# Decode attention kernel: the latent cache is loaded with four tokens to a partition, 3 KB a piece on 32 partitions, instead of one token to a partition

## The chip, the cores and the metric

The kernel runs on one core of one Trainium2 chip. The metric is the device time of one execution in microseconds (us). Engine names are those of the profile: PE is the matrix engine, PEld its weight loads, DVE, ACT and POOL are the vector, scalar and general engines, and SP is the engine that does nothing here but issue transfers (SPq in the rows).

## What is computed

One layer of a hybrid decoder, for a prompt of 1,024 tokens and for eight decode sequences ("rows" of a batch; here called sequences) of four new tokens each, over a past of 2,048 tokens that lies in a paged cache. Of this only the second attention of the decode matters for the change. Its cache holds 192 numbers for a token, 128 of a latent vector and 64 of a rotated key, and page_table says which 16 pages of 128 tokens a sequence owns:

```
past_mla = cache_mla_l[page_table].reshape(Bd, PAST_LEN, KV_LORA + ROPE_DIM)
full_mla = jnp.concatenate([past_mla, mla_row], axis=1)
o_lat = mla_attend(q_lat, q_rope, full_mla[..., :KV_LORA], full_mla[..., KV_LORA:], pos, ...)

def mla_attend(q_lat, q_rope, ckv, k_rope, q_pos, k_pos):
    s = (jnp.einsum('bthr,blr->bhtl', q_lat, ckv)
         + jnp.einsum('bthe,ble->bhtl', q_rope, k_rope)).astype(jnp.float32) * scale
    p = masked_softmax(s, (k_pos[None, :] <= q_pos[:, None])[None, None])
    return jnp.einsum('bhtl,blr->bthr', p.astype(ckv.dtype), ckv)
```

All 2,048 past tokens are visible to every new token, and no term of the score depends on where a past token stands. So the sum over past tokens may be taken in any order, if scores and values use the same one.

## The kernel before

The program is written engine by engine, with semaphores between them. It runs the prompt first (projection, attention, output projection, to about 880 us of the span), then the eight decode sequences one after the other, in a loop over `b` on each engine, and a short output projection for the decode at the end. There is no scheduler: each engine runs its instructions in the order in which the code lists them.

All loads of the decode are issued by SP. For a sequence `b` SP waits until sequence `b - 2` has been finished on PE (semaphore `s_avd`), since the two buffers of each kind alternate (`b % 2`). Then it issues in this order: 16 pages of the other cache (`load_pages`, 256 KB each, into `NSA`), the state of the window (`load_window`, 512 KB, into `WND`), 256 KB of prepared queries (`load_keyed`), 16 pages of the latent cache (`load_latent`, 96 KB each, into `MLD`), and two stores of the window (`store_window`). The page's number is read from a register, so each page has a transfer and some register work of its own. For sequence 0 the same functions are called from the output projection of the prompt (`sp_out`), `load_latent` in its tile 5.

`MLD[b % 2]` has for each of 128 partitions 16 slots of 192 numbers. Two places read it. On DVE, `latent_turns(b)` (L2796) waits for all 16 transfers (`s_ml`) and then turns blocks of 32x32 of it into `MLT` for the scores, by three instructions; it stands in DVE's order behind the last copy of compressor chunks of sequence `b` (L2725, chunk V3), and the whole softmax work of sequence `b` is queued behind it. PE needs its result in `latent_scores` (L2592). On PE, `latent_values` (L2631) multiplies slot `n` of `MLD` by column block `n` of the probabilities, on all 128 partitions. Both take slot and partition as they come: the score of the token in slot n of partition p ends in place (n, p) of the probabilities, and meets the same slot and partition in `latent_values`.

The other cache is needed at its first chunk: PE's `chunk(b, "K0")` (L2339) waits for the 16 transfers of `load_pages`, and stands in PE's order behind the selected scores (L2605) of the sequence before.

Of the kernel before, what the change touches and what calls it, by code (L numbers as in the profile page):

```python
# [20 lines left out]
P = 128  # L21
# [93 lines left out]
def build(nc, x_prompt, x_sample, cache_nsa, cache_mla, state_win, page_table, c_prompt, c_sample,  # L115
# [3 lines left out]
    with ExitStack() as ctx:  # L119
# [34 lines left out]
        def view(off, n):  # L154
            return AR[:, off:off + n]
# [1415 lines left out]
        for u, (kind, i, half, heads, k0, nb, og) in enumerate(UNITS):  # L1571
# [5 lines left out]
            n = len(CH_OF[u])  # L1577
# [454 lines left out]
        def sp_out(sp, tiles, at):  # L2032
            for m, j in enumerate(tiles, at):
                if m >= 2:
                    sp.wait_ge(s_g2, 2 * (m - 1))
                if m >= 1:
                    sp.dma_start(XO[m % 2][0:rows(j), :], x_t[j]).then_inc(s_xo[m % 2], 16)
                if m == 1:
                    load_bias(sp)
                if m == 2:  # L2040
                    load_queries(sp)
                    load_compressors(sp)
                    load_gates(sp)
                if m == 3:
                    pages = page_numbers(sp, 0)
                    load_pages(sp, 0, pages, 0, 8)
                if m == 4:
                    load_pages(sp, 0, pages, 8, NPG)
                if m == 5:
                    load_latent(sp, 0, pages)  # L2050
                if 3 <= m <= 6:
                    keyed_store(sp, m - 3)
                if m == 6:
                    load_keyed(sp, 0)
                    load_window(sp, 0)
                    store_window(sp, 0)
                if m > at:
                    sp.wait_ge(s_yo, m)
                    sp.dma_start(y_t[tiles[m - 1 - at]], YO[(m - 1) % 2][0:rows(tiles[m - 1 - at]), :])\
                        .then_inc(s_out[(m - 1) % 2], 16)  # L2060
# [152 lines left out]
        MLD = [view(o, 3072).rearrange("p (n c) -> p n c", n=NPG) for o in (16384, 38304)]  # L2213
# [266 lines left out]

        def load_latent(sp, b, pages):
            for n in range(NPG):
                sp.dma_start(MLD[b % 2][:, n, :], cache_mla[0, bass.ds(pages[n], 1)].rearrange("o t c -> (o t) c"))\
                    .then_inc(s_ml[b % 2], 16)

        def load_window(sp, b):
# [11 lines left out]
        def sp_decode(sp):  # L2498
            load_mask(sp)
            for b in range(1, NB):  # L2500
                pages = page_numbers(sp, b)
                if b == 1:
                    sp.wait_ge(s_yT, NT)
                load_pages(sp, b, pages, 0, NPG)
                if b == 1:
                    load_late(sp)
                    sp.wait_ge(s_yo, NT)
                    sp.dma_start(y_t[NT], YO[1]).then_inc(s_out[1], 16)
                load_window(sp, b)
                load_keyed(sp, b)  # L2510
                load_latent(sp, b, pages)
                store_window(sp, b)
            sp.wait_ge(s_avd, 8 * (NB - 2) + 8)
            load_weights(sp, WOUT2)
            sp.wait_ge(s_r, 2 * NB)
            for c in range(4):
                at, cs = RS * c, slice(256 * c, 256 * c + 256)
                for b in range(NB):
                    sp.dma_start(GPS[at + TS * b:at + TS * b + TS, :], gate_dram[b:b + 1, cs].to_broadcast([TS, 256]))\
                        .then_inc(s_gps, 16)  # L2520
                sp.dma_start(XOS[at:at + RS, :], x_t[0][:, cs]).then_inc(s_gps, 16)
                sp.dma_start(GFS[at:at + RS, :], g_final[256 * c:256 * c + 256].rearrange("(o n) -> o n", o=1)
                             .to_broadcast([RS, 256])).then_inc(s_gps, 16)
# [540 lines left out]
```

## Time and profile before

| | |
|---|---|
| median of 3 runs | 1114.52 us (1111.03 to 1114.62) |
| profiled execution, its own time | 1115.21 us |
| its span in the trace | 1113.2 us |
| mean granted clock of PE | 0.991 of full speed |
| busy: PE, DVE, ACT, POOL | 97%, 56%, 33%, 8% of the span |
| moved by DMA | 120.25 MB, 108 GB/s over the span |

The profile is of one execution. The span is the time from its first to its last instruction; the execution's own time is 2.0 us longer. Start times in rows count from the start of the span. "Landing" of a transfer counts from its issue to its last byte. A DMA share is the mean busy share of the core's 16 DMA engines; in a short window it can read slightly over 1.

### The profile page before, as it was taken

To read this page: it belongs to the slowest core of one execution; us is meant where nothing else is said; L and a number is where in the kernel's file an instruction comes from. 1 tells how busy PE (TensorE), PEld (TensorE's weight loads), DVE (VectorE), ACT (ScalarE), POOL (GpSimd) and SP (SyncE) were. 2 spreads that over 40 slices of the span, in tenths; PEclk is the share of its full clock that TensorE was granted. 3 is DMA by queue.
4 is the path that set the end of the run, shared out by engine and by line. 5 is a ranking of instruction groups with operands and counts; after the bars stand their busy time and mean duration, and the time that the engine had idled before them with its cause. 6 is when DMAs were issued, how large, how long until landed. Compare 5 with 4: busy or idle time off the path is not lost. (4 is left out here: it accounts for less than half of the span.)

```text
span 1113.2 us, 22587 instructions
## 1 busy us (share of the span) xinstructions
PE 1075.2 (97%) x8368; PEld 763.3 (69%) x8368; DVE 624.6 (56%) x1627; ACT 362.5 (33%) x893; POOL 86.5 (8%) x184
## 2 busy tenths in 40 slices
PE   6899999999999999998999999999999999999997
PEld 3455599998886677776776657664544576777775
DVE  0645323463423477769677766742323588888883
ACT  0322001121112475546555555631112133333330
POOL 0210100110000011101101010011000200000000
PEclk9899999999999999999999999999999999999998
DMA  9933270001006240000000000005794467878781
GB/s 355 310 115 94 72 211 2 16 19 72 1 1 122 44 116 2 1 1 2 1 2 1 2 1 2 1 1 119 169 307 152 142 217 262 271 274 275 261 251 51
DMA packets 96612, 120.25 MB, mean 108 GB/s; under 512 B 31569, under 2 KB 65380, under 8 KB 95480
## 3 DMA queue, kind: packets, MB, share of 16 engines
q1 hardware_dynamic: 96504, 118.81, 34.4%
q8 instruction: 68, 1.11, 0.4%
q14 instruction: 40, 0.33, 0.1%
HBM read 104.41 MB, written 14.36 MB: 107 GB/s over the span
## 5 line engine op out<-in xcount | busy, mean ns | idle before, releaser
L549 PE MATMUL PS<-AR 128*128 128x256 f32 (+2 forms) x896 | 219.7, 403 | 0.0
L549 PEld LDWEIGHTS PS<-AR 128*128 128x128 f32 x896 | 167.8, 190 | 45.2 <-issue 6.2
L2090 PE MATMUL PS<-AR 128*128 128x512 f32 x256 | 112.3, 592 | 0.0
L1747 PE MATMUL PS<-CA,AR 128*128 128x128 f32 x704 | 111.4, 282 | 0.8 <-ACT AR L1821 0.8
L963 DVE TENSOR_TENSOR AR<-PS,AR 128x256 f32<-128x256 f32 (+2 forms) x80 | 36.2, 452 | 134.4 <-PE PS L549 134.3
L1747 PEld LDWEIGHTS PS<-CA,AR 128*128 128x128 f32 x704 | 77.0, 143 | 44.6 <-issue 31.7
L1821 ACT ACTIVATE AR<-PS 128x512 f32<-128x512 f32 (+1 forms) x108 | 58.2, 546 | 125.1 <-PE PS L1747 124.5
L1725 PE MATMUL PS<-AR 128*128 128x65 f32 (+1 forms) x688 | 89.3, 271 | 0.0
L2090 PEld LDWEIGHTS PS<-AR 128*128 128x128 f32 x256 | 47.5, 190 | 54.0 <-issue 54.0
L1725 PEld LDWEIGHTS PS<-AR 128*128 128x128 f32 x688 | 84.3, 192 | 0.0
L1806 ACT ACTIVATE AR<-PS,SM_ 128x512 f32<-128x512 f32 (+4 forms) x192 | 76.6, 471 | 15.9 <-DVE SM_ L1914 8.8
L1700 PE MATMUL PS<-AR 64*128 64x512 f32 (+3 forms) x384 | 74.1, 491 | 6.6 <-ACT AR L1803 3.9
L1835 DVE COPY AR<-PS 128x512 f32<-128x512 f32 (+1 forms) x100 | 57.3, 586 | 15.5 <-PE PS L1747 15.1
L1803 ACT ACTIVATE AR<-PS,SM_ 128x512 f32<-128x512 f32 (+2 forms) x80 | 51.5, 655 | 15.4 <-DVE SM_ L1914 15.3
L760 ACT ACTIVATE AR<-PS 128x256 f32<-128x256 f32 (+2 forms) x20 | 8.0, 402 | 139.7 <-PE PS L549 98.6
L1876 DVE TENSOR_REDUCE SM_<-PS 128x1 f32<-128x512 f32 (+1 forms) x48 | 29.9, 664 | 41.8 <-PE PS L1696 30.2
L1722 PE MATMUL PS<-AR 128*64 128x128 f32 x656 | 50.0, 282 | 1.2 <-DVE AR L1980 1.2
L2183 DVE TENSOR_TENSOR AR<-PS,AR 128x512 f32<-128x512 f32 x16 | 11.1, 692 | 71.0 <-PE PS L2090 71.0
L541 PE MATMUL PS<-AR 128*64 128x128 f32 x896 | 49.8, 273 | 0.0
L541 PEld LDWEIGHTS PS<-AR 128*64 128x64 f32 x896 | 48.8, 137 | 1.3 <-issue 1.2
L1992 POOL TENSOR_TENSOR AR<-AR 128x256 f32<-128x256 f32 x32 | 23.3, 727 | 326.3 <-DVE AR L1980 325.7
L1700 PEld LDWEIGHTS PS<-AR 64*128 64x128 f32 x384 | 28.9, 185 | 26.3 <-ACT AR L1803 11.9
(364 smaller groups left out, 1622.9 us busy)
## 6 DMA issues: line engine op xcount, KB each, us to landing
AR<-in_cache_nsa SPq DMA_DIRECT2D x128, 256.0 KB, 5.0
AR<-in_cache_mla SPq DMA_DIRECT2D x128, 96.0 KB, 3.7
AR<-in_x_prompt SPq DMA_DIRECT2D x16, 512.0 KB, 4.6
AR<-in_w_ada SPq DMA_DIRECT2D x3, 2048.0 KB, 11.4
AR<-in_w_in SPq DMA_DIRECT2D x6, 1024.0 KB, 8.4
AR<-in_w_ada SPq DMA_DIRECT2D x8, 512.0 KB, 4.3
AR<-in_w_out SPq DMA_DIRECT2D x4, 1024.0 KB, 10.0
AR<-in_w_out SPq DMA_DIRECT2D x2, 2048.0 KB, 17.5
```

The costliest lines, as they stand in the source:

```text
L541: mm = pe.matmul(bank[64 * h:64 * h + 64, P * r:P * r + P], weights[:, k, h, 64 * r:64 * r + 64], tokens[:, k, :], start=(fresh and r == 0 ...
L549: mm = pe.matmul(bank[:, 0:WIDE[g]], tokens[:, k, :], w, start=(fresh and k == 0), stop=(last and k == 3), skip_group_check=True)
L963: return dve.tensor_tensor(out, src, other, ALU.add)
L1700: mm = pe.matmul(scores(u, gi, o, o + P * n), QT[64 * g:64 * g + 64, r, q], keys[64 * g:64 * g + 64, ks], start=True, stop=True)
L1722: mm = pe.matmul(ob[64 * g:64 * g + 64, P * (r % 2):P * (r % 2) + P], (VS1 if kind == "sel" else VW1)[:, kb, g, 0:64], tile, start=(n == 0 ...
L1725: mm = pe.matmul(out, tile, v, start=(n == 0), stop=(n == nb - 1))
L1747: mm = pe.transpose(PS[:, 4 + c % 2, P * (t - t0):P * (t - t0) + P], tile(u, t), ident)
L1803: act.activation(probs(u, gi, lo, hi), sc, ACT.Exp, bias=NM[:, at, gi:gi + 1], scale=-1.0, accum_out=TOT[og % 4][:, slot:slot + 1]).then_i ...
L1806: act.activation(probs(u, gi, lo, hi), sc, ACT.Exp, bias=NM[:, at, gi:gi + 1], scale=-1.0).then_inc(s_exp, 1)
L1821: evac(act, c, lambda o, i: act.activation(o, i, ACT.Copy), s_evA)
L1835: copy(PTB[:, c % 4, 0:nt, :], PS[:, 4 + c % 2, 0:P * nt].rearrange("p (t q) -> p t q", t=nt)).then_inc(done, 1)
L2090: mm = pe.matmul(PS[0:n, 2 + 2 * (m % 2) + c, :], YTO[m % 2][:, f, 0:n], weights[:, f, 512 * c:512 * c + 512], start=(f == 0), stop=(f == 7))
```

## The change

Each page of the latent cache, 128 tokens of 768 bytes that lie one behind the other, was written one token to a partition, into slot n. Now tokens 4h to 4h+3 of page n go to one partition, 4h + n % 4, into the four slots from 4 (n // 4) on. These slots are neighbours, so that the four tokens are one piece of 3,072 bytes on both sides. A transfer has 32 such pieces in place of 128 of 768 bytes, and writes every fourth partition; four pages (n, n+1, n+2, n+3 of one group) together fill the same four slots of all 128 partitions. Nothing else is changed: the same 128 transfers of 96 KB, the same buffer, the same semaphore and count.

```
         def load_latent(sp, b, pages):
             for n in range(NPG):
-                sp.dma_start(MLD[b % 2][:, n, :], cache_mla[0, bass.ds(pages[n], 1)].rearrange("o t c -> (o t) c"))\
+                sp.dma_start(MLD[b % 2][n % 4:P:4, 4 * (n // 4):4 * (n // 4) + 4, :],
+                             cache_mla[0, bass.ds(pages[n], 1)].rearrange("o (h l) c -> (o h) l c", l=4))\
                     .then_inc(s_ml[b % 2], 16)
```

In SP's order, at the loads for sequence 1, the program before reads as follows (AR is the one large on-chip array of which MLD, WND and NSA are views, in_cache_mla is the latent cache; an ISA row is the register work for a page's address, and 128x192 are partitions and numbers of a partition):

```order
L2489 DMA AR<-in_state_win 128x1024
L2387 DMA AR<-sample_q_by_key_weights 128x512
L2483 ISA
L2483 DMA AR<-in_cache_mla 128x192
L2483 ISA
L2483 DMA AR<-in_cache_mla 128x192
```

and the changed program, at the same place:

```order
L2490 DMA AR<-in_state_win 128x1024
L2387 DMA AR<-sample_q_by_key_weights 128x512
L2483 ISA
L2483 DMA AR<-in_cache_mla 32x768
L2483 ISA
L2483 DMA AR<-in_cache_mla 32x768
```

No instruction moved; SP has 712 such rows in both, with the shape of the latent transfers as their only difference. Lines behind L2483 are one higher in the changed program.

In DVE's order, at the turns of sequence 0's latents, the changed program has the rows of the program before (there they are L2725, L2812, L2796, L2833 and L2834), with the same shapes:

```order
L2726 COPY AR<-PS 128x32x16
L2813 STREAM_TRANSPOSE AR<-AR 128x4x4x32
L2797 STREAM_TRANSPOSE AR<-AR 128x16x2x32 x3
L2834 TENSOR_SCALAR AR<-AR 32x127
L2835 TENSOR_TENSOR AR<-PS,CE 128x128
```

Nothing moved here either; the three instructions that wait for the latent transfers read the same 128 partitions and 16 slots.

## Rows read from the trace of the kernel before

**Rows 1.** The page: engines, and the span in 40 slices.

```profile
PE 1075.2 (97%) x8368; PEld 763.3 (69%) x8368; DVE 624.6 (56%) x1627; ACT 362.5 (33%) x893; POOL 86.5 (8%) x184
...
DMA  9933270001006240000000000005794467878781
```

**Rows 2.** Waits, whole span: of seven that name a DMA, largest and smallest.

```profile
engine line waited for: us in total, times, longest us
...
ACT AR L880 <- DMA AR<-in_x_prompt: 23.0, 3, 16.2
...
PE PS L648 <- DMA AR<-in_w_in: 1.7, 1, 1.7
```

**Rows 3.** Waits of DVE alone, 740 to 1113 us, some of twenty.

```profile
DVE AR L2864 <- PE PS L2598: 6.4, 7, 0.9
...
DVE AR L2725 <- PE PS L2339: 5.5, 14, 0.5
```

**Rows 4.** Chain that ended last, one sequence: start, us, engine and line.

```profile
938.54 1.09 PE PS L2543 x64
...
942.33 3.63 PE PS L2592 x8
...
965.01 1.09 PE PS L2543 x64
```

**Rows 5.** SP's timeline, loads for sequences 3 and 4: start, us, line, count.

```profile
938.66 8.66 SPq L2478 DMA_DIRECT2D AR<-in_cache_nsa  x16
947.38 0.43 SPq L2489 DMA_DIRECT2D AR<-in_state_win  x1
947.86 0.43 SPq L2387 DMA_DIRECT2D AR<-sample_q_by_key_weights  x1
948.48 9.14 SPq L2483 DMA_DIRECT2D AR<-in_cache_mla  x16
957.68 0.94 SPq L2495 DMA_DIRECT2D out<-AR  x2
964.68 9.70 SPq L2478 DMA_DIRECT2D AR<-in_cache_nsa  x16
```

**Rows 6.** The readers of these loads, timeline: PE's K0 chunk, DVE's turns.

```profile
957.25 0.60 PE L2339 MATMUL PS<-CA,AR 128*128 128x128 f32 x4
...
965.05 1.08 DVE L2725 COPY AR<-PS 128x512 f32<-128x512 f32 x1 [0.45 <-PE PS L2339]
...
965.98 1.22 DVE L2796 STREAM_TRANSPOSE AR<-AR 128x1024 f32<-128x1024 f32 x1
```

**Rows 7.** Issues and landings of the latent and of the other cache.

```profile
L2483 SPq DMA_DIRECT2D AR<-in_cache_mla x128: 332/333/1355, 823.3 to 1064.6; - x128
...
DMA to landing us min/median/max: 1.9/3.7/6.5
...
L2478 SPq DMA_DIRECT2D AR<-in_cache_nsa x128: 332/333/1692, 802.9 to 1054.6; - x128
...
DMA to landing us min/median/max: 2.6/5.0/7.4
```

**Rows 8.** Windows: us, engines busy, and last granted clock, DMA share, GB/s.

```profile
938.66:960.60 21.94, 21.94 (x245) 15.39 (x230) 17.94 (x42) 4.52 (x10) 1.54 (x3) 1.00 0.95 323
960.60:964.60 4.00, 3.54 (x56) 3.10 (x55) 3.89 (x8) 3.98 (x6) 0.00 (x0) 1.00 0.03 8
...
1045.14:1067.90 22.76, 22.76 (x221) 16.20 (x208) 18.70 (x46) 5.94 (x13) 0.00 (x0) 1.00 0.91 311
```

**Rows 9.** Windows in which one kind of load leads, same columns.

```profile
824.00:832.00 8.00, 8.00 (x23) 3.80 (x22) 1.38 (x2) 0.60 (x1) 0.00 (x0) 1.00 0.82 242
...
784.00:786.00 2.00, 2.00 (x36) 1.07 (x35) 1.03 (x2) 0.00 (x0) 0.00 (x0) 1.00 1.06 182
...
845.90:848.50 2.60, 2.60 (x8) 1.17 (x7) 0.00 (x0) 0.00 (x0) 0.00 (x0) 1.00 0.86 301
911.67:920.80 9.13, 9.13 (x100) 5.73 (x99) 7.98 (x16) 0.88 (x3) 0.00 (x0) 1.00 0.88 291
```

**Rows 10.** DVE's copy of a chunk with no load in flight, timeline.

```profile
963.02 1.06 DVE L2725 COPY AR<-PS 128x512 f32<-128x512 f32 x1
```

## The prediction

> **What bounds the kernel now.** I first read the page. PE is busy for 97% of the span, and the DMA engines are loaded only in parts, with shares of 0.7 to 0.8 in the decode [rows 1]. A load that is shared out so can still be a bound at one place, so the next view is the list of waits: what ended the idle time of an engine. Seven entries name a DMA, and all seven are of the projection in the first part of the span, on x, w_ada, w_in and a constant; the largest is 23.0 us and the smallest 1.7 us [rows 2]. None names the latent cache, and none is of the decode. DVE, which alone waits for the latent transfers directly, waited in the loop over sequences for PE and ACT: at L2864 seven times, 0.9 us at most, and at L2725 0.5 us at most [rows 3]; L2796, where the latents are waited for, is not in the list.
>
> The third view is the chain that ended last. Through a sequence of the decode it goes from PE instruction to PE instruction with a few on DVE, and it repeats: PE's key products start at 938.54 and again at 965.01, so a sequence takes 26.47 us [rows 4]. No transfer stands in it.
>
> The fourth view is SP and the queue, since a hidden load is hidden by a margin, and the change acts on the margin. For one sequence SP issues from 938.66 to 958.62, and the loads of the next sequence start at 964.68 [rows 5]. SP idles some 6 us, waiting for PE to free a buffer. The DMA engines work at a share of 0.95 until 960.60, and then at 0.03 for 4.00 us [rows 8]. So of 26.0 us between the starts of two bursts the queue is full for 21.94, and has 4.1 us to spare; in the last burst it is full for 22.76.
>
> **What the change does, part by part.**
>
> *Issue on SP.* There are as many transfers and register instructions as before. An issue is 332 to 333 ns in the median [rows 7], the same for 128x192 and for 128x512 numbers, so it doesn't follow the size. The 16 take 9.14 us [rows 5], or 0.57 us each with the register work. I take no change. If a transfer of fewer pieces were cheaper to issue, SP would idle longer before its next wait; if each cost 0.3 us more, the 16 would cost 4.8 us, which the 6 us still hold. Both give 0 us on the path. SP's queue behind the latents holds only the two window stores, and then the wait for PE.
>
> *The transfers.* The latents are 16 x 98,304 bytes = 1.57 MB for a sequence. What they cost the queue now is best seen at sequence 0, where they are issued with little else in flight: 242 GB/s at a share of 0.82 in 8.00 us [rows 9], that is 1.94 MB for 6.56 us of full queue. In it is one load of x, 0.52 MB in 4 KB pieces; such pieces move 301/0.86 = 350 GB/s at full share [rows 9], so it takes 1.5 us, and 1.42 MB of latents take 5.1 us: 280 GB/s, or 5.6 us of queue for a sequence. The pieces now are 3,072 bytes, between the 2 KB of the other cache, 291/0.88 = 331 GB/s [rows 9], and 4 KB at 350. By size alone they would take 4.5 to 4.75 us, about 1 us less. That is the gain side. The loss side is the shape, 32 partitions in place of 128. The nearest row has loads onto 32 partitions in pieces of 512 bytes: 182 GB/s at a share of 1.06, 172 at full share [rows 9]. It mixes smaller pieces with fewer partitions and doesn't tell them apart. At that rate the latents take 9.1 us, 3.5 us more. I take the gain side for the size, since the pieces here are much nearer to 2 and 4 KB and step over all 128 partitions where those of the row lie together, and keep both ends: -1.1 to +3.5 us of queue for a sequence.
>
> *What that is worth on the path.* With the gain, the queue is empty at 959.6 in place of 960.60. Nothing then starts earlier: the next burst waits for PE, and the readers come later. DVE's turns start at 965.98, right behind a copy that began at 965.05 and takes 1.08 us [rows 6]; they didn't wait for data that was there by 960.60. The gain is 0 us. With the loss of 3.5 us all is in at 964.1, still before 964.68 and before the turns at 965.98: also 0 us. The next in danger would be PE's first chunk of the other cache. The last of its pages is issued by 947.3 [rows 5] and lands within 7.4 us [rows 7], by 954.4 at the latest; it is read at 957.25 [rows 6], 2.8 us later. A burst that leaves work over for the next eats from these 2.8 us first. In the last burst, full for 22.76 us, nothing urgent follows.
>
> *Readers.* DVE's three turns and PE's matmuls read the same addresses, 128 partitions and 16 slots, with the same shapes. A token's score and its value sit in the same partition and slot as each other. 0 us.
>
> *Sequence 0.* Its latents are issued at 823.3 and needed only when the decode starts, near 880 us. 0 us.
>
> The sum is 0 us. Against the profiled execution that gives 1115.2 us (span 1113.2 and 2.0 around it). The median of the runs is 0.7 us under it, so I predict 1114.5 us as the median.
>
> The Trainium skill has a rule that bears on this, in SBUF — State Buffer, section "Door 1: The DMA port swizzle": a transfer's rate goes by how many of 16 ports its partitions reach, partitions 0 to 31 reach only eight (189 GB/s against 328 for 128 partitions, at 1 MiB), and bits 2 to 4 and 6 of the partition's number choose the port. The row with 32 partitions agrees in direction (172 against 331 to 350 GB/s), small pieces included. By that rule, partitions in steps of four reach all 16 ports, two pieces each, so it foresees no loss for this stride; by its general advice to use 128 partitions the rate would be some 189/328 of before, an estimate, and the latents would cost 9.7 us of queue in place of 5.6.
>
> **Rivals.**
>
> *The pieces collide, and the latents move at half rate.* For it speaks the row at 172 GB/s; against it, that those pieces are of 512 bytes and on neighbouring partitions. Half of 331 GB/s makes 9.5 us of queue in place of 5.6: +3.9, against 4.1 us of spare time. The queue is just full. In bursts of 22.8 us, like the last, it would carry 0 to 1 us over to the next; over six gaps that is up to 5 us, of which the margin of 2.8 us at the other cache takes the first part. That gives 0 to +3 us, 1114.5 to 1117.5. Chance 0.12; a quarter of it ends above 0.3%. (The advice in SBUF — State Buffer of the Trainium skill, were it to hold for this stride, is this case.)
>
> *The queue becomes the bound: slower.* If the 32 pieces of a transfer were dealt to only four of the 16 DMA engines, the latents would move at a quarter of 331 GB/s, 19.0 us a sequence, +13.4. Less 4.1 us of spare time that is 9.3 us for each of six gaps between the seven bursts: +56 us, less the 2.8 once, 1168 us. It decides from +4.1 us on, that is, when the latents cost more than 9.7 us. DVE would then wait at L2797 for the latents, with the whole softmax queued behind it. Against it: the loads onto 32 partitions at 784 us kept a share of 1.06 over all 16 engines [rows 9], so transfers of 32 partitions do use them all. Chance 0.03.
>
> *Transfers disturb the engines, and fewer pieces disturb less: faster.* DVE's chunk copy takes 1.06 us with no load in flight [rows 10] and 1.08 us as a burst starts [rows 6]. If all of 0.02 us in 1.06 were such disturbance, 2%, and the change took away all that the latents cause (9.14 of 26.47 us), it would give 0.7% of the decode of 230 us, 1.6 us: 1113. To be visible it would have to be twice that. Chance 0.05, of which 0.03 visible; and I give 0.02 to a gain that the views don't show.
>
> *The change does less than it says.* If the pieces were cut again to 768 bytes in the queue, everything stays as it was: also no change, and part of the forecast.
>
> **How the numbers follow.** The forecast, hidden on both sides, has a chance of 0.78 at 1114.5. The runs of before differ by 0.3% among themselves, 1111.03 to 1114.62, and 0.3% or 3.3 us is about what a measurement here can tell from none. Range: 1110.0 to 1119.0. Its low end is the fastest run less 1 us, or the disturbance rival with that scatter; the high end is the half rate's 1117.5 with 1.5 us of scatter. The quarter rate lies outside. Faster by over 0.3%: 0.05, slower 0.08 (0.03 from the half rate, 0.03 from the bound queue, 0.02 from scatter), within 0.3%: 0.87.
>
> **What would show it.** Right: no entry of the waits in the decode names in_cache_mla; a sequence in the chain still takes 26.4 to 26.5 us; about 12,300 packets fewer (128 transfers, 96 fewer each); the queue in the burst at 939 empty at or before 960.6, by about 1 us; issue of 332 to 333 ns unchanged. Wrong on the size, though not on the time: queue full until 962 to 965. Wrong: DVE idle before L2797 with a DMA as releaser, or PE idle before the K0 chunk; a period above 27 us; or fewer than 16 engines used, seen as a DMA share near 0.25 or 0.5 in the middle of the latents.

## The result and the profile after

The changed kernel takes 1124.21 us in the median of 8 runs (1119.27 to 1127.07), the kernel before 1114.57 us beside it (8 runs, 1110.57 to 1117.61). The ratio is 1.0087, with a 95% interval of 1.0061 to 1.0112: 9.6 us slower. The forecast was no change, in a range that ended at 1119.0. The profiled execution took 1126.05 us, with a span of 1124.0 us.

The page of the changed kernel, answering [rows 1]:

```profile
PE 1079.5 (96%) x8368; PEld 766.9 (68%) x8368; DVE 624.9 (56%) x1627; ACT 361.8 (32%) x893; POOL 87.0 (8%) x184
...
DMA  9932260020006320000000000006874666677792
```

The engines do the same work as before, and the DMA engines are less loaded in the decode, not more. The key products of sequences 1, 2 and 7 on PE in the changed kernel (start, us):

```profile
913.24 1.16 PE L2544 MATMUL PS<-AR 64*32 64x128 f32 x64
939.70 1.16 PE L2544 MATMUL PS<-AR 64*32 64x128 f32 x64
...
1083.37 1.16 PE L2544 MATMUL PS<-AR 64*32 64x128 f32 x64
```

From sequence 2 to sequence 7 that is 143.67 us, against 132.34 us before (938.48 to 1070.82): 11.3 us more. The spans differ by 10.8, so the loss lies in this stretch. The waits of the changed kernel have an entry of the decode that names a DMA, which [rows 2] had not:

```profile
PE PS L2339 <- DMA AR<-in_cache_nsa: 7.1, 5, 2.4
```

PE waits at its K0 chunk, and for the other cache, whose transfers nobody touched. The latents are waited for nowhere. So the question is what made those pages late. SP's timeline for sequences 3 and 4, answering [rows 5]:

```profile
943.85 9.30 SPq L2478 DMA_DIRECT2D AR<-in_cache_nsa  x16
953.20 0.42 SPq L2490 DMA_DIRECT2D AR<-in_state_win  x1
953.67 0.43 SPq L2387 DMA_DIRECT2D AR<-sample_q_by_key_weights  x1
954.30 11.92 SPq L2483 DMA_DIRECT2D AR<-in_cache_mla  x16
966.27 1.08 SPq L2496 DMA_DIRECT2D out<-AR  x2
973.47 9.07 SPq L2478 DMA_DIRECT2D AR<-in_cache_nsa  x16
```

The 16 latent transfers take SP 11.92 us, where they took 9.14; over the bursts of sequences 2 to 7 it is 11.4 us in the mean against 8.9. And although SP finishes with the stores only at 967.35, the next burst again starts 6.1 us later. That gap was read as idle time ahead of a wait for PE. The chain of the changed kernel goes through it, and shows what it is (start, us, line; rows of "issue" between them left out):

```profile
966.89 0.46 SPq L2496
...
967.40 1.85 SPq L2470
969.28 0.16 SPq L2470
...
969.54 0.15 SPq L2470
969.80 0.15 SPq L2470
...
973.07 0.15 SPq L2470
...
973.47 0.37 SPq L2478
```

L2470 is `page_numbers`: one load of 16 numbers into SP's registers, and register work with a range check for each. The timeline, which lists what is counted as an engine's work and the transfers, leaves them out. They stand in the kernel before as well, for the same burst, in the answer for that line from 957 to 966 us:

```profile
L2470 SPq FUSED_REGOPS  x16: 147/147/157, 960.5 to 964.3; - x16
L2470 SPq SEQ_ASSERT  x16: 18/18/18, 960.7 to 964.5; - x16
L2470 SPq TENSOR_LOAD <-PT_SB x1: 1797/1797/1797, 958.7 to 958.7; - x1
```

From 958.7 to 964.5 of the 6.06 us, SP was at work. PE's last product that frees the buffer (L2655) ended at 964.42, just before, so the burst looked as if it had waited for it. The list of SP's own waits for the kernel before, from 880 us on, has one wait for PE at the head of a burst:

```profile
SPq L2478 <- PE PS L2655: 2.2, 1, 2.2
```

It lies ahead of sequence 2's burst at 911.67. After it SP never waited for PE again, and its bursts started 26.0 to 27.0 us apart, 26.69 in the mean, where PE's work takes 26.47. So SP had no spare time before the change, not 6 us of it. It was slightly the slower of the two, and only the margin hid it: the last page of the other cache landed 4.5 us before its K0 chunk at sequence 2, and 2.1 us before it at sequence 7. In the changed kernel the list of SP's waits has no such entry. Issues and landings in the changed kernel, answering [rows 7], say where the added time is:

```profile
L2483 SPq DMA_DIRECT2D AR<-in_cache_mla x128: 472/472/1687, 826.1 to 1080.7; - x128
...
DMA to landing us min/median/max: 2.1/2.8/6.4
...
L2478 SPq DMA_DIRECT2D AR<-in_cache_nsa x128: 332/333/851, 805.8 to 1068.4; - x128
```

A latent transfer's issue holds SP for 472 ns in place of 333. Sixteen of them are 2.2 us more for each sequence, on an engine that had nothing to spare. The two stores right behind the latents, whose shape is unchanged, went from 451 to 531 ns in the median as well. The landing of a latent is shorter than before, 2.8 us against 3.7.

### The profile page after: what moved, and what is told of

Read it like the earlier page. It is cut to its first block and busy times, and to the rows that moved or that the text cites. A ratio compares the mean times of both kernels' runs of the same rounds, so it can differ in the third digit from the quotient of the medians.

```text
span 1124.0 us, 22587 instructions
## 1 busy us (share of the span) xinstructions
PE 1079.5 (96%) x8368; PEld 766.9 (68%) x8368; DVE 624.9 (56%) x1627; ACT 361.8 (32%) x893; POOL 87.0 (8%) x184
```

## Experiments

In all of them the issue is the median duration of the latent transfer's instruction on SP, and the period is the mean distance of the starts of SP's bursts from sequence 2 to 7 (five distances): 26.69 us before, 28.99 us in the changed kernel. Ratios are to the kernel before, with 95% intervals. A version without a ratio has a single run. The kernel before took 1110.3 to 1120.0 us in its runs beside these experiments, so a single time inside that stretch tells nothing, and such versions are read for their issues; 1123.4, 1125.6 and 1128.0 us further down lie above it.

### 32 partitions that lie together

```
-                sp.dma_start(MLD[b % 2][n % 4:P:4, 4 * (n // 4):4 * (n // 4) + 4, :],
+                sp.dma_start(MLD[b % 2][32 * (n % 4):32 * (n % 4) + 32, 4 * (n // 4):4 * (n // 4) + 4, :],
```

> The changed kernel, with page n on 32 partitions that lie together (32 (n % 4) on) in place of every fourth one; pieces of 3,072 bytes as there. Theory A (SP is what lasts longest for a sequence, and an issue of 472 ns in place of 332 ns makes it late): the time follows the length of the issue and nothing else. If the partition step makes the issue long, it is 332 ns here and the time is that of before, 1114 to 1116 us; if the size or number of pieces does, 472 ns and 1122 to 1126 us. Theory B (the DMA engines move pieces on 32 partitions slowly): no faster than the changed kernel, and slower still if partitions that lie together share ports, 1124 us and more, with landings of the latents above 3.7 us in the median.

1114.88 us, ratio 1.0002 (0.9977 to 1.0026). The latents in this kernel:

```profile
L2483 SPq DMA_DIRECT2D AR<-in_cache_mla x128: 315/316/1592, 823.2 to 1063.5; - x128
...
DMA to landing us min/median/max: 2.0/5.5/7.4
```

The pieces, their size and their number are those of the changed kernel; only the step is gone, the issue is 316 ns, the period 26.47 us, and the whole loss is gone with it. At the same time the transfers themselves are slower than in either kernel: a median landing of 5.5 us, twice that of the changed kernel. So the kernel with the slow transfers is the fast one, and theory B falls. The landings are what the Trainium skill's SBUF — State Buffer, section "Door 1: The DMA port swizzle", leads one to expect: by it, 32 partitions that lie together reach eight ports and those in steps of four all sixteen. The trace agrees in the landings; for the time it made no difference. The two landings are not a clean price of the ports, since the transfers of the version with the longer issue also follow one another more slowly. At nearly equal issues (467 and 472 ns) the landing was 3.5 us on every second partition of one half, a version further down, and 2.8 us on every fourth partition.

### Two tokens to a partition, with and without a step

```
-                sp.dma_start(MLD[b % 2][n % 4:P:4, 4 * (n // 4):4 * (n // 4) + 4, :],
-                             cache_mla[0, bass.ds(pages[n], 1)].rearrange("o (h l) c -> (o h) l c", l=4))\
+                sp.dma_start(MLD[b % 2][n % 2:P:2, 2 * (n // 2):2 * (n // 2) + 2, :],
+                             cache_mla[0, bass.ds(pages[n], 1)].rearrange("o (h l) c -> (o h) l c", l=2))\
```

> The changed kernel with two tokens to a partition: 64 pieces of 1,536 bytes on every second partition. Theory A: the time follows the issue; if the issue grows with partitions per transfer or piece size in steps it is between 332 and 472 ns, at 400 ns some 1.1 us a sequence less on SP than in the changed kernel, 1116 to 1120 us; if any step other than one partition costs 140 ns, 472 ns and 1122 to 1126 us. Theory B: in the middle as well, by the number of partitions, with landings in the middle.

1123.51 us, ratio 1.0091 (1.0058 to 1.0125), an issue of 475 ns, a period of 29.10 us. The loss is that of the change, not half of it. I read this as "any step costs", and tried the same on 64 neighbouring partitions, `MLD[b % 2][64 * (n % 2):64 * (n % 2) + 64, ...]`:

> The run with two tokens to a partition, on 64 partitions that lie together: the same 64 pieces of 1,536 bytes, no step. If the step is the price (474 against 315 ns was seen with 32 partitions), the issue is 310 to 335 ns and PE doesn't wait for the other cache, 1111 to 1118 us. If 64 partitions or half-full transfers are the price, 470 ns and about 1123 us.

```profile
L2483 SPq DMA_DIRECT2D AR<-in_cache_mla x128: 468/469/1694, 823.1 to 1079.6; - x128
```

One run gave 1125.6 us (before, beside it: 1114.8). The issue is 469 ns without any step. "Any step costs" does not explain this one.

### Small pieces on the same 32 partitions

```
-                             cache_mla[0, bass.ds(pages[n], 1)].rearrange("o (h l) c -> (o h) l c", l=4))\
+                             cache_mla[0, bass.ds(pages[n], 1)].rearrange("o (l h) c -> (o h) l c", l=4))\
```

> The changed kernel, with tokens h, 32 + h, 64 + h and 96 + h of a page in partition 4h + n % 4: the same 32 partitions in steps of four, but 128 pieces of 768 bytes as before the change. Tells the size of the piece from the partitions. Theory A: an issue of about 472 ns if the partitions make it long, 1122 to 1126 us; about 332 ns if the 3 KB pieces do, then 1114 to 1116 us; longer than 472 ns if a third dimension costs something of its own, then above 1126 us. Theory B by partitions: 1124 us with slow landings; by piece size: 1114 us.

1136.25 us, ratio 1.0206 (1.0180 to 1.0233), and a period of 30.50 us:

```profile
L2483 SPq DMA_DIRECT2D AR<-in_cache_mla x128: 602/602/1220, 821.9 to 1088.1; - x128
...
DMA to landing us min/median/max: 2.2/2.8/6.7
```

The issue is 130 ns longer than in the changed kernel. Two things differ, a third dimension and 128 pieces in place of 32, and no run here parts them; the kernel before, with 128 pieces in two dimensions and no step, has 333 ns. The landing is as in the changed kernel with a quarter of the piece's size, though the transfers also follow one another more slowly. The loss is 22.5 us where the issue is 269 ns dearer than before, and 9.6 where it is 139 ns dearer: the time grows with the issue. In this version DVE waited for the latents too, 1.8 us in two waits.

### Less work on SP

```
-                PT_SB[0:1, NPG * b:NPG * b + NPG], engines=[mybir.EngineType.SP], min_val=0, max_val=NPHYS - 1)
+                PT_SB[0:1, NPG * b:NPG * b + NPG], engines=[mybir.EngineType.SP], min_val=0, max_val=NPHYS - 1,
+                skip_runtime_bounds_check_because="a page table holds pages of the cache")
```

> The changed kernel, with SP's work between two bursts cut: the range check of the sixteen page numbers of a sequence is left out (the numbers are loaded into registers as before, without a test that each is a page of the cache), which takes the register rows of L2470 away, some 4 us a sequence. The latent transfers and their issue stay as in the changed kernel. Theory A: SP has 4 us more than it needs to make up the 2.2 us, PE no longer waits for the other cache, and the time is that of before or up to 2 us below it: 1112 to 1116 us, with an issue of 472 ns all the same. Theory B: SP waits for the DMA engines anyway, so nothing changes: 1122 to 1126 us.

1114.04 us, ratio 1.0002 (0.9985 to 1.0019), a period of 26.47 us. The latents are loaded exactly as in the changed kernel, and their issue is unchanged:

```profile
L2484 SPq DMA_DIRECT2D AR<-in_cache_mla x128: 472/472/1367, 822.0 to 1063.9; - x128
```

With 4 us less of SP work elsewhere, the loss is gone. Now SP does wait for PE, as this kernel's list of SP's waits shows (once in the kernel before, never in the changed one):

```profile
SPq L2479 <- PE PS L2657: 12.9, 6, 5.0
```

The same with the 32 neighbouring partitions, both edits together:

> Pieces of 3 KB on 32 partitions that lie together, with the page numbers unchecked: SP gets the cheaper issue (315 ns) and loses the 4 us of the range check. Theory A: SP waits for PE by 4 to 5 us a sequence, and since PE then paces the decode by itself nothing is gained over before: 1112 to 1116 us. A gain below 1111 us would show that SP's timing cost something in the kernel before too.

1114.19 us, ratio 0.9999 (0.9974 to 1.0024). Room on SP beyond what it needs gains nothing; no version here is faster than the kernel before by more than the scatter.

### More work on SP, with the latents as before

```
                 load_latent(sp, b, pages)
+                for k in range(7):
+                    sp.dma_start(tiny_dram[7 * (b - 1) + k:7 * (b - 1) + k + 1, :], c_prompt[0:1, 0:16]).then_inc(s_tiny, 16)
                 store_window(sp, b)
```

> The kernel before, with seven transfers of 64 bytes (from memory to memory, to places of their own that nobody reads) issued on SP behind the latents of each of sequences 1 to 7. The latent loads are those of before. At some 0.3 us each they take SP 2.1 to 2.4 us a sequence, about what the change adds with 16 times 0.14 us, and the DMA engines next to nothing. Theory A (SP paces the decode): the loss of the change is reproduced, 1121 to 1127 us, and PE waits for the other cache at the K0 chunk. Theory B (the transfers themselves, or what they do to the engines): 1113 to 1116 us.

1157.4 us, ratio 1.0410 (1.0355 to 1.0465). The mechanism is as expected and the size isn't, since I had the price of a tiny transfer too low:

```profile
L2515 SPq DMA_DIRECT2D tiny<-in_c_prompt x49: 528/590/3736, 900.6 to 1100.7; - x49
```

Seven of them took SP 4.3 to 7.5 us a sequence, not 2.1 to 2.4. PE waited 24.6 us for the other cache at its K0 chunk. With three in place of seven:

> As the run with seven, with three transfers of 64 bytes a sequence: some 1.0 us more on SP. SP's bursts of before are 26.7 us apart, against 26.47 us of PE's work, and the first margin is 2.8 us. Theory A: 1.0 us times six is 6 us, less the margin and what SP had to spare: 0 to 4 us slower, 1114 to 1118 us. Theory B: 1113 to 1116 us.

1125.84 us, ratio 1.0112 (1.0073 to 1.0151), a period of 29.21 us. That is outside the 1114 to 1118 us expected, again by the price: three took SP 1.8 us in most bursts and 2.9 in one, not 1.0. This is the closest copy of the change: about 2 us of issue a sequence, next to nothing for the DMA engines, 128x192 latents, and its loss is 12.1 us with this wait:

```profile
PE PS L2341 <- DMA AR<-in_cache_nsa: 8.4, 4, 2.8
```

### What makes an issue dear

First without a register address, on the load of the window's state, cut in two in the kernel before:

```
-            sp.dma_start(WND[b % 2][:, :, :].rearrange("p j c -> p (j c)"),
-                         state_win[0, b].rearrange("(p j) c g d -> p (j c g d)", j=4)).then_inc(s_wn[b % 2], 16)
+            for o in range(2):
+                sp.dma_start(WND[b % 2][o:P:2, :, :].rearrange("p j c -> p (j c)"),
+                             state_win[0, b].rearrange("(p j) c g d -> p (j c g d)", j=4)[o:P:2]).then_inc(s_wn[b % 2], 16)
```

(the other run has `64 * o:64 * o + 64` for `o:P:2`; the counts that are waited for grow with the third transfer).

> The kernel before, with the load of the window's state (a fixed address, 4 KB pieces) cut in two: even partitions and odd ones, 64 each in steps of two. It measures the issue of a stepped transfer without a register address. If the partition step costs 0.14 us by itself, these two have issues of 0.46 us and more, against 0.32 to 0.34 us at the least for the same halves without a step; if it costs only with an address from a register, both forms are alike.

> The same cut in two halves of neighbouring partitions, 0 to 63 and 64 to 127: as many transfers, pieces and bytes as in the run with even and odd partitions, no step. Issues of 0.32 to 0.43 us, as other transfers with fixed addresses have; the difference of the two runs is the price of the step.

The issues are 591 and 578 ns, against 432 ns for the same 128 partitions in one transfer; the times are 1113.6 and 1116.6 us (before, beside them: 1110.9), and PE waited 3.9 us at K0 in the second and not at all in the first. Without a step 0.32 to 0.43 us was expected, so this is a miss: 64 partitions are dear here without a step, and a step of two adds 13 ns. Nor do these issues price the shape alone. The load of the queries stands right behind, and nobody touched it; its issue, in the kernel before and in the one with neighbouring halves:

```profile
L2387 SPq DMA_DIRECT2D AR<-sample_q_by_key_weights x8: 320/434/829, 845.1 to 1055.4; - x8
...
L2387 SPq DMA_DIRECT2D AR<-sample_q_by_key_weights x8: 320/583/586, 845.5 to 1060.9; - x8
```

So a part of what a dear shape costs SP shows in the issue of the transfer behind it. Then the latents at fixed addresses (`cache_mla[0, n:n + 1]` for `cache_mla[0, bass.ds(pages[n], 1)]`), once with the step of four and once on neighbouring partitions:

> The changed kernel, with the latents of every sequence read from pages 0 to 15, at fixed addresses, in place of those that the page table names (so the latent part of the decode is that of other tokens; everything else is as it was). The step of four partitions stays, the register goes. If the step costs SP only together with an address from a register, the issue is as long as in its twin without a step; if the step costs by itself, it is 140 to 160 ns longer than there. The register rows of the 16 pages go too (some 0.18 us each), so by theory A SP has room again and the time is 1111 to 1118 us in either case.

> The twin: latents from pages 0 to 15 at fixed addresses (the same part of the computation is that of other tokens), on 32 partitions that lie together. It gives the issue of a fixed-address transfer of 32x768 without a step; 315 to 430 ns by other fixed-address loads. Time 1111 to 1118 us.

594 and 422 ns, 1117.1 and 1113.5 us in one run each (before, beside them: 1114.8). The step costs 172 ns without a register too. The room that the missing register work was expected to give, 16 times 0.18 or 2.9 us, hardly came: with the step the 16 latents held SP for 10.8 us in the mean of the bursts of sequences 2 to 7, against 11.4 with a register, and PE waited 4.1 us at K0. By these times what the register work had taken is now inside the longer issue, so an issue with a fixed address is to be set only against another one with a fixed address. Last, three forms to tell a step from a span over several groups of 32 partitions, the first with four tokens to a partition (l=4) and the others with eight (l=8):

```
+                sp.dma_start(MLD[b % 2][64 * (n % 2) + n // 2 % 2:64 * (n % 2) + 64:2, 4 * (n // 4):4 * (n // 4) + 4, :],
+                sp.dma_start(MLD[b % 2][32 * (n % 4) + n // 4 % 2:32 * (n % 4) + 32:2, 8 * (n // 8):8 * (n // 8) + 8, :],
+                sp.dma_start(MLD[b % 2][16 * (n % 8):16 * (n % 8) + 16, 8 * (n // 8):8 * (n // 8) + 8, :],
```

> The changed kernel, with page n on 32 partitions in steps of two, inside the 64 partitions of one half; pieces of 3,072 bytes. What makes an issue 470 ns long? By the span: a transfer is dear if its partitions lie in more than one group of 32 without filling all 128 (both forms on 64 partitions and the step of four were). By the step: any step makes it dear, and 64 partitions do for another reason. Both say 470 ns here; 315 ns would refute both. Time by the issue: 1120 to 1127 us at 470 ns.

> Eight tokens to a partition, 16 pieces of 6,144 bytes on every second one of 32 partitions that lie together. By the span: inside one group of 32, so the issue is as cheap as in its twin without a step, near 315 ns. By the step: 470 ns. Time 1111 to 1117 us at the cheap issue, 1120 to 1127 us at the dear one.

> The twin: 16 pieces of 6,144 bytes on 16 partitions that lie together. Both the span and the step say a cheap issue near 315 ns, and 1111 to 1117 us if the landings, on fewer partitions, stay within PE's margin; a dear issue here would say that it is the number of partitions (32 or 128 against others) that decides.

1123.4, 1128.0 and 1112.5 us in one run each (before, beside them: 1113.5). The first has an issue of 467 ns. The issue with 16 partitions in steps of two:

```profile
L2483 SPq DMA_DIRECT2D AR<-in_cache_mla x128: 509/510/1477, 822.8 to 1080.4; - x128
```

and with 16 neighbouring ones:

```profile
L2483 SPq DMA_DIRECT2D AR<-in_cache_mla x128: 315/316/1403, 825.2 to 1065.0; - x128
```

The time of the second is 1 us above the range expected for a dear issue, with an issue of 510 ns where 470 was expected. A step inside one group of 32 costs 194 ns, so the span falls as the whole cause. All forms of a latent transfer of 96 KB, in one table:

| partitions | pieces | address | issue, step 1 | issue, stepped |
|---|---|---|---|---|
| 128 | 128 of 768 B | register | 333 ns | |
| 64 | 64 of 1,536 B | register | 469 | 475 (step 2) |
| 32 | 32 of 3,072 B | register | 316 | 467 (step 2), 472 (step 4) |
| 32 | 128 of 768 B | register | | 602 (step 4) |
| 16 | 16 of 6,144 B | register | 316 | 510 (step 2) |
| 32 | 32 of 3,072 B | fixed | 422 | 594 (step 4) |

A step costs 151 to 194 ns wherever the form without one is cheap. Why 64 neighbouring partitions are dear where 16, 32 and 128 are cheap stays open; no run here tells it, nor why a step is dear.

## Why the prediction was wrong

**The step that failed** is the first, "Issue on SP", with both things that it took as given: the price of an issue, and the room that SP had for a dearer one. It took 332 to 333 ns for the new shape, from "the same for 128x192 and for 128x512 numbers, so it doesn't follow the size". Those two rows share the number of partitions and have no step, and could say nothing on a stepped transfer. The measured issue is 472 ns.

It then had a bound for just this case, "if each cost 0.3 us more, the 16 would cost 4.8 us, which the 6 us still hold". The measured price was half of that, and it did not hold. "SP idles some 6 us, waiting for PE to free a buffer" was read from a timeline with nothing in it between two transfers; the rows of L2470 fill 958.7 to 964.5 of them, and SP did not wait for PE there. In the kernel before SP needed 26.69 us a sequence in the mean against PE's 26.47, so its spare time was nil. With that the same bound gives a loss. The changed kernel's period of 28.99 us is 2.5 us above PE's, 12.6 us over the five periods from sequence 2 to 7. The last page of sequence 2 was 2.3 us early, so some 10.3 us are left. Measured: 11.3 us in the profile between the key products of these sequences, and 9.6 us between the medians.

**The transfers.** Their term, -1.1 to +3.5 us of queue with the gain side taken, had the sign right. The packets of the latents alone, summed from the traces between 900 and 1060 us, took the 16 engines 3.29 us for each MB before and 2.99 in the changed kernel, or 5.2 and 4.7 us a sequence: 0.5 us less, where the term said 1.1. On 32 neighbouring partitions they took 4.00, or 6.3 us. The view of the DMA queues over the same stretch gives for the main queue packets, MB and share. In the kernel before:

```profile
q1 hardware_dynamic: 28762, 41.03, 76.0%
```

In the changed kernel:

```profile
q1 hardware_dynamic: 18516, 37.45, 68.3%
```

With 32 neighbouring partitions:

```profile
q1 hardware_dynamic: 20683, 41.58, 81.3%
```

For each MB of all loads that is 1.85, 1.82 and 1.96 points. The packets over the whole span fell by 12,288, as forecast. The gain in queue time is small, and worth nothing on the path, also as forecast.

**The path.** The place was named in the prediction: "PE idle before the K0 chunk" and "a period above 27 us" stand among the signs of being wrong, and its margin of 2.8 us at the other cache. (By its own figures that margin is 2.6 us, since 947.3 and 7.4 make 954.7; in the trace this burst's last page landed 3.3 us early.) Only the cause that it allowed, a queue left full, was the wrong one; the burst was late because its issuer was.

**The rivals.** Half rate: no; the latents' packets took less time for each MB, not twice as much. Queue as the bound: no; its share fell from 76.0% to 68.3%. Disturbance of the engines: no; with SP relieved, the kernel with 32 pieces a transfer is as fast as the one before, not faster. None of them had SP as the pacing engine, though its bursts were 26.0 to 27.0 us apart in the rows. The range ended at 1119.0 since it took its upper end from the queue alone.

**What PE's waits do not show.** PE waited 7.1 us and lost 11.3. The rest is for the most part its clock. In the changed kernel, around the wait of 2.42 us before 988.54, the windows read (granted clock third from the end):

```profile
987.00:990.00 3.00, 1.46 (x24) 1.32 (x28) 0.95 (x2) 0.79 (x1) 0.75 (x1) 0.88 1.04 398
990.00:993.00 3.00, 3.00 (x42) 2.48 (x33) 0.16 (x1) 0.38 (x2) 0.00 (x0) 0.55 0.68 236
```

and the latent values right behind it ran at

```profile
989.10 1.81 PE L2632 MATMUL PS<-AR 128*32 128x128 f32 x32
```

instead of 1.08 us. A mean of 0.55 of full speed over 3 us is mostly time at 1.2 in place of 2.4 GHz; PE had stood idle for 2.42 us before. After the wait of 1.95 us the mean was 0.65 (1046.2 to 1050.0); after those of 0.84, 0.81 and 1.12 us it stayed at 1.00. But this is not an extra loss while SP paces. The K0 chunks that waited start at 959.47, 988.54, 1017.63, 1046.24 and 1075.64, 28.6 to 29.4 us apart, after waits of 2.42 and of 0.81 us alike: a slow stretch uses up the next wait. I conclude this from the rows; no run kept the clock up to try it.

## What to carry to other kernels

A transfer's price has a part on the engine that issues it, and here that part followed the shape, not the bytes: 256 KB pages and 96 KB latents both had 333 ns on 128 partitions, and 96 KB had 316 to 602 ns by its form. Where one engine issues many transfers in a loop, sum its whole loop, address loads and range checks included, and set it against the loop of the engine it feeds; a timeline that shows only transfers makes a full issuer look idle. Before reshaping a transfer for better pieces, look for a row of the same form (partitions, step, dimensions); here 3 KB pieces on neighbouring partitions cost nothing, and the same pieces on every fourth partition cost 0.9% of the kernel.

## What was unexpected of the hardware

A partition step of two or four in the on-chip side of a transfer lengthened its issue from 316 to between 467 and 510 ns, 128 small pieces in a third dimension by another 130 ns, and 64 neighbouring partitions needed 469 ns without a step. A part of such a price fell on the next transfer, whose own shape was unchanged (434 to 583 ns). The shape with the shortest issue (32 neighbouring partitions, 316 ns) had nearly the slowest landing (5.5 us), and the changed kernel's, with a long issue, one of the fastest (2.8 us).

Loading 16 page numbers into SP's registers with a range check took 5.8 us in the burst shown, of which the load is 1.8. Without the checks only the load's row is left at that line, so the other 4.0 us are the checks.

The Trainium skill says in DMA: Bandwidth & Descriptors, section "Issuing engines are not separate DMA queues", that the sequencer's time for starting a transfer is usually small relative to the transfer. For a single latent that holds here, 0.47 us against a landing of 2.8 us. But landings overlap and issues of one engine do not: SP was held for 11.4 us by 16 latent transfers whose packets took 4.7 us of the 16 engines, so in a row the measurement differs, and it decides the time.
